# A decoder step on one NeuronCore: other orders ahead of the expert loop (sample numerators, gate rows, per-layer-embedding turns)

## Chip, cores and metric

The kernel runs on one core of one Trainium2 chip. The metric is the device time of one execution in microseconds (us), the median of several runs. All data are float32 in HBM.

## The reference, cut to what matters

One layer of a hybrid decoder for 512 prompt tokens and 8 x 8 sample tokens (576 tokens, width 1024): an mLSTM mixer with 4 heads beside a pooling mixer, then 64 routed experts (8 per token) and one shared, then a per-layer embedding (PLE) behind a gate.

```python
def _layer(x, p, C0, n0, m0, buf0, start_pos, ...):
    h = _rmsnorm(x, norm_mix_g)
    z = h @ w_in                                   # q, k, v, o, gates i and f, u
    i_pre = z[..., g0:g0+H] + b_igate;  log_f = log_sigmoid(z[..., g0+H:g0+2*H] + b_fgate)
    h_a, C, n, m = _mlstm(q * DH**-0.5, k, v, i_pre, log_f, C0, n0, m0)
    h_a = headnorm(h_a) * head_norm_g * sigmoid(o)
    h_b, buf = _pool_mixer(u, buf0, start_pos, w_pool, pool_scale)
    x = x + concat(h_a, h_b) @ w_out
    x = x + _moe(_rmsnorm(x, norm_ffn_g), ...)     # 64 experts of (1024x256, 1024x256, 256x1024), top 8
    gate = sigmoid(_rmsnorm(x, norm_ple_g) @ w_ple_gate)
    return x + (p @ w_ple_proj) * gate, C, n, m, buf
# _mlstm, for a token t after a stored state (C0, n0, m0), the sample tokens' case:
#   num = w_inter * (q C0) + (scores * decay) v ;  nq = w_inter * (q n0) + rowsum(scores * decay)
#   h = num / max(|nq|, exp(-m_t)) ;  C = fw * C0 + sum_s iw_s k_s v_s
```

## The kernel before, in words

The program is written out by hand, engine by engine (SyncE issues loads and stores, GpSimd, ScalarE, VectorE, TensorE), with semaphores between them. Ahead of the expert loop TensorE's work is a list of groups. Each group of matrix products fills one of the eight PSUM banks, and one engine, VectorE ("v") or ScalarE ("s"), drains it. `psum_groups` lists all groups in the order in which TensorE fills them; group n has bank n mod 8 (`free_bank` waits until group n-8 is drained, `full_bank` until group n is filled), and `drain` asserts that each engine drains its groups in the order of the list. So an order is changed in three places: the list, TensorE's program and the draining engine's program.

The stages ahead of the loop, as far as the change touches them:

- 0 to 19 us. x comes in by five tiles (four of 128 tokens, one of 64), is turned (`x1T`), and ScalarE and GpSimd work out rstd of each token and diagonals of it. A product of ones with the diagonals spreads rstd over all partitions: `rB` 0 for the prompt tiles, `rB` 1 for the sample tile (L2003). Then come the gate rows `g` (L2012) and q, k, u (L1978), whose weights come through a ring of two chunks of 2 MB. VectorE waits for both spreads and then works the gate rows out ahead of its drains of q.
- 199 to 230 us. Behind the prompt's numerators `num`: `Ms` (rows spread over partitions, L2088), `Ss` (the sample scores), the turns of k (`kn`, L2098) and `kns`, the turn `n0` of the stored normaliser, the prompt states `Cp` (L1978, 128x129), which need k weighted by VectorE (L1475), the turns of the gated heads (`haT`, L2111), which need `head_out` on VectorE (L1502, L1504), and the output product `wo` (L1978, 128x512). VectorE's chain in front of `head_out` goes over GpSimd once (L908). The sample numerators `nS` (L2201, 72 pairs of instructions) need only `Ms`, `Ss`, `n0` and the loaded states; they stand behind `wo`(0,1), the last prompt state and the third `haT`. ScalarE copies them and takes four squares. After `wo`(0,1) the norm of x2 tile 0 runs over ScalarE, GpSimd and VectorE (L1299), and `turn_x`(0) (L1973) on TensorE waits for it.
- 318 to 343 us. The router has chosen the experts of each token. From sorted positions VectorE builds one-hots (L1733 to L1753), a product with them picks the rows of one loop step (`pick`, L2269), VectorE turns this into row numbers (`first_index`, L1768 to L1778), and GpSimd gathers the rows from HBM by four indirect DMAs (L994). VectorE transposes the gathered rows (`turned_rows`, L1786). In between run the shared expert's first products of tiles 2 and 3 (`first`, L2155), its product on GpSimd or, for the last tile, on VectorE (L1810), the turns of that (`turn_h`, L2164), and ten transposes of the PLE input (`pT`, L2291), which ScalarE drains (L1172) once `s_order` is 2, as their target holds routing data until then. SP loads the third expert's weights (home 4: `mixpj`, `wide`, L666 and L670), whose place holds the PLE input, after the last `pT` drain; home 3 (`xT`) after the last `first`(3).
- The loop: 46 steps of up to 128 gathered rows, each with one to two experts. A step's first product (L2314, L2319) needs the transposed rows and the weights; its end releases a place for the next expert's weights (3 MB each). TensorE enters it when the last eight groups are drained, `pk` 2 (VectorE) and `shT` 3 (ScalarE) among them. The tail after it holds the PLE gate and the final norm.

## Time and profile before

| | us |
|---|---|
| median of 3 runs | 1022.5 |
| lowest and highest | 1021.36, 1022.6 |
| the profiled execution | 1020.37 |
| its span | 1018.3 |
| mean granted TensorE clock, share of full | 0.984 |
| TensorE busy | 959.6 |
| VectorE, ScalarE, GpSimd busy | 426.8, 146.4, 344.5 |
| DMA moved | 297.50 MB, mean 292 GB/s |

Times in the rows are microseconds from the start of the span. A row of a timeline is: start, duration, engine, line, operation, output <- input, shape, count, and in brackets the idle time of the engine ahead of it with what released it. PE is TensorE's matmul, PEld its weight load, DVE VectorE, ACT ScalarE, POOL GpSimd, SPq a DMA issued by SyncE. A row of the windows is: stretch and its length; busy time and instructions of PE, PEld, DVE, ACT and POOL; granted clock; DMA share; GB/s. A row of the chain of waits is: start, duration, what was on the chain. Each TensorE product of float32 makes two rows of count.

### The profile page before, as it was taken

What the parts mean: (1) busy time and instruction counts of PE and PEld (TensorE: products, weight loads), DVE (VectorE), ACT (ScalarE), POOL (GpSimd) and SP (SyncE); (2) the same over time, 40 slices, a digit from 0 to 9 for tenths busy, and PEclk for the clock granted to TensorE, in tenths of its full rate; (3) what the DMA queues carried; (4) which work ended last, traced back from release to release, by engine and by line L of the source; (5) the groups of instructions that cost most, each with busy time, mean ns of one, the idle gap of its engine ahead of it and who ended that gap; (6) DMA issues with size and microseconds to landing.
All of it is one profiled execution on the core that took longest, in us unless ns stands there. A gap on an engine that the chain in (4) does not pass through costs nothing.

```text
span 1018.3 us, 16186 instructions
## 1 busy us (share of the span) xinstructions
PE 959.6 (94%) x5994; PEld 420.7 (41%) x5994; DVE 426.8 (42%) x1215; ACT 146.4 (14%) x358; POOL 344.5 (34%) x439
## 2 busy tenths in 40 slices
PE   7999999999999899999999998989997899989996
PEld 5777655555554433233222333323332223333442
DVE  3411222344578543344343342333424243432885
ACT  4000023401011101010110000000100001102332
POOL 6000321310143644444344443334433344440132
PEclk9999999999999899999999999999998999999998
DMA  8032214222067999999999999999999999988932
GB/s 275 10 94 104 83 63 131 85 73 64 38 235 275 362 349 399 411 409 413 412 413 413 405 415 413 410 393 397 411 410 399 380 409 411 412 328 341 421 136 83
DMA packets 76115, 297.50 MB, mean 292 GB/s; under 512 B 15622, under 2 KB 26062, under 8 KB 49149
## 3 DMA queue, kind: packets, MB, share of 16 engines
q1 hardware_dynamic: 60133, 258.68, 65.0%
q0 software_dynamic: 15904, 37.79, 9.7%
q8 instruction: 48, 0.79, 0.3%
q14 instruction: 30, 0.25, 0.1%
HBM read 276.56 MB, written 31.50 MB: 303 GB/s over the span
## 4 chain that ended last, share of the span: by engine, by line
PE 64%; DMA 22%; DVE 5%; issue 4%; POOL 3%; DVEq 1%; SPq 1%; ACT 1%; POOLq 0%; ACTq 0%
PE bank L1978 22%; PE bank L2319 18%; DMA arena<-in_ex_w 9%; PE bank L2314 7%; DMA arena<-xs_dram,slot 6%; PE bank L2414 5%; DMA ring<-in_ex_w 5%; PE bank L1984 2%; PE bank L2155 2%; POOL arena L994 2%; DMA arena<-y_dram 1%; PE bank L2082 1%; PE bank L2072 1%; DMA x<-in_x_prompt 1%; PE bank L2119 1%
## 5 line engine op out<-in xcount | busy, mean ns | idle before, releaser
L2319 PE MATMUL bank<-arena 128*32 128x512 f32 x1440 | 270.4, 608 | 10.6 <-issue 4.7
L994 POOL DMA_INDIRECT arena<-xs_dram,slot x192 | 204.8, 1066 | 73.1 <-issue 62.3
L2319 PE MATMUL bank<-ring,arena 128*32 128x512 f32 x864 | 212.2, 605 | 5.8 <-DMA arena<-in_ex_w 5.8
L1010 POOL DMA_INDIRECT y_dram<-arena,outrow x46 | 47.1, 1023 | 270.3 <-DVE slot L1772 214.3
L2319 PE MATMUL bank<-xT,arena 128*32 128x512 f32 x576 | 114.7, 604 | 5.5 <-DMA ring<-in_ex_w 5.5
L2319 PEld LDWEIGHTS bank<-arena 128*32 128x32 f32 x1440 | 68.0, 112 | 112.5 <-issue 104.3
L1786 DVE STREAM_TRANSPOSE arena<-arena 128x1024 f32<-128x1024 f32 x48 | 59.7, 1244 | 87.2 <-DMA arena<-xs_dram,slot 87.1
L1978 PE MATMUL bank<-xT,ring 128*128 128x288 f32 x384 | 93.4, 407 | 0.0
L2319 PE MATMUL bank<-mixpj,arena 128*32 128x512 f32 x384 | 86.4, 599 | 0.0
L1978 PEld LDWEIGHTS bank<-xT,ring 128*128 128x128 f32 x384 | 73.0, 190 | 20.4 <-DMA ring<-in_w_in 0.5
L2319 PEld LDWEIGHTS bank<-ring,arena 128*32 128x32 f32 x864 | 51.0, 111 | 49.9 <-issue 43.9
L1851 DVE SCALAR_TENSOR_TENSOR arena<-bank,gate,arena 128x256 f32<-128x256 f32 x46 | 22.2, 484 | 110.8 <-ACT arena L1204 110.7
L1832 DVE COPY outrow<-yrow 128x1 int32<-128x1 int32 x46 | 7.1, 154 | 146.8 <-PE bank L2319 117.6
L1204 ACT ACTIVATE arena<-bank 128x256 f32<-128x256 f32 x46 | 17.7, 384 | 345.1 <-PE bank L2319 259.4
L1978 PE MATMUL bank<-ring,mixpj 128*128 128x512 f32 x128 | 56.7, 597 | 0.8 <-issue 0.8
L1978 PE MATMUL bank<-ring,xT 128*128 128x512 f32 x128 | 56.1, 593 | 0.0
L2414 PE MATMUL bank<-ring,xT 128*128 128x512 f32 x128 | 55.7, 593 | 0.4 <-DVE xT L1903 0.4
L2314 PE MATMUL bank<-ring,arena 128*128 128x512 f32 (+1 forms) x112 | 51.9, 614 | 1.3 <-DVE arena L1786 1.3
L1200 ACT COPY arena<-bank 128x512 f32<-128x512 f32 x46 | 27.0, 587 | 174.7 <-PE bank L2319 137.1
L2314 PE MATMUL bank<-arena 128*64 128x512 f32 x144 | 50.2, 596 | 0.7 <-DVE arena L1833 0.6
L2319 PEld LDWEIGHTS bank<-xT,arena 128*32 128x32 f32 x576 | 29.1, 111 | 50.2 <-issue 43.4
L886 POOL TENSOR_TENSOR arena<-arena 128x710 f32<-128x710 f32 (+3 forms) x10 | 13.9, 1394 | 94.7 <-DVE arena L1391 87.8
(417 smaller groups left out, 1242.5 us busy)
## 6 DMA issues: line engine op xcount, KB each, us to landing
arena<-in_ex_w SPq DMA_DIRECT2D x78, 1024.0 KB, 21.7
ring<-in_ex_w SPq DMA_DIRECT2D x50, 1024.0 KB, 20.4
xT<-in_ex_w SPq DMA_DIRECT2D x28, 1024.0 KB, 19.1
mixpj<-in_ex_w SPq DMA_DIRECT2D x24, 1024.0 KB, 20.1
arena<-y_dram SPq DMA_DIRECT2D x18, 1024.0 KB, 11.0
wide<-in_ex_w SPq DMA_DIRECT2D x12, 1024.0 KB, 25.4
ring<-in_w_in SPq DMA_DIRECT2D x5, 2048.0 KB, 8.2
ring<-in_w_out SPq DMA_DIRECT2D x2, 2048.0 KB, 8.5
```

Source lines behind the costliest of these rows:

```text
L994: pool.indirect_dma_start(xg[b][:, 256 * a:256 * a + 256], None, xs_quarter, bass.IndirectOffsetOnAxis(slot[k][:, a:a + 1], 0), bounds_che ...
L1010: pool.indirect_dma_start(y_dram, bass.IndirectOffsetOnAxis(outrow[b][:, 0:1], 0), og[b], None, bounds_check=K * T - 1, oob_is_err=False). ...
L1200: act.copy(og[b][:, 0:512], bank[5][:, :]).then_inc(s_out0, 1)
L1204: act.activation(hs, bank[2][:, 0:FF], ACT.Silu).then_inc(s_silu, 1)
L1786: dve.transpose(xgT[b][:, :, :].rearrange("p c (a t) -> p a c t", t=32), xg[b].rearrange("p (a c t) -> p a c t", c=KT, t=32)).then_inc(s_x ...
L1851: dve.scalar_tensor_tensor(out=hh, in0=bank[2][:, FF:2 * FF], scalar=gate[depth(j)][:, 0:1], in1=hs, op0=ALU.mult, op1=ALU.mult).then_inc( ...
L1978: ins = pe.matmul(b, lhs(c), rhs(c), start=(c == 0), stop=(c == nk - 1))
L1984: pe.matmul(b[0:NS, 0:n], lhs(c), rhs0(c), start=(c == 0), stop=(c == nk - 1))
L2155: ins = pe.matmul(b[0:r, :], xT[:, c, tok(i)], sw13[:, :, c, :], start=(c == 0), stop=(c == KT - 1))
L2314: ins = pe.matmul(b[t, :], lhs[:, t], rhs(home(p)), start=start, stop=stop)
L2319: ins = pe.matmul(b[t, :], lhs[:, t], rhs(home(own if lane < 3 else common)), start=start, stop=stop)
L2414: ins = pe.matmul(bank[AT["gt", i, n] % 8][0:r, :], xT[:, c, tok(i)], w[:, c, :], start=(c == 0), stop=(c == KT - 1))
```

## The change

Three reorderings. No instruction is added or removed.

1. The gate rows `g` come between the two spreads `rB` 0 and `rB` 1.
2. `n0` is turned and drained ahead of `Ms`. `nS` comes right behind `kns`, ahead of the prompt states; of `Ss` it waits only ahead of its last step. The turn of k 3 and prompt state 2 come ahead of `wo`(0,0). ScalarE copies and squares `nS` ahead of the prompt states; VectorE weights k 3 ahead of `head_out`(1).
3. The five `pT` groups come ahead of the first pick, and ScalarE drains them ahead of the turn of the sample tile's shared product. The last `first`(3) is cut after three of eight products instead of two. VectorE transposes the first gathered rows (`turned_rows(64, 0)`) ahead of its shared product of the last tile and of `first_index(2)`, instead of behind them.

```diff
--- before.py
+++ after.py
@@ -41,7 +41,7 @@
     g = [(("g1",), "v")]
     for i in range(NT):
         g += [(("x1T", i, 0), "v"), (("x1T", i, 1), "v")]
-    g += [(("rB", 0), "s"), (("rB", 1), "s"), (("g",), "v")]
+    g += [(("rB", 0), "s"), (("g",), "v"), (("rB", 1), "s")]
     g += [(("q", j, n), "v") for j in range(H) for n in range(2)]
     g += [(("k", j, n), "v") for j in range(H) for n in range(2)]
     g += [(("u", j, n), "v") for j in range(H) for n in range(2)]
@@ -57,7 +57,7 @@
         if h == 0:
             g += [(("o", NT - 1), "s")]
         g += [(("num", h, i), "s") for i in range(4)]
-    g += [(("Ms", 0), "v"), (("Ms", 1), "v"), (("Ss",), "v")]
+    g += [(("n0",), "v"), (("Ms", 0), "v"), (("Ms", 1), "v"), (("Ss",), "v")]
 
     def halves(key, i, e):
         return [((key, i, n), e) for n in range(1 if i == NT - 1 else 2)]
@@ -68,19 +68,19 @@
     def state(h):
         return [(("C", h, c), "v") for c in range(3)]
 
-    g += [(("kn", 0), "v"), (("kn", 1), "v"), (("kns",), "s"), (("n0",), "v")]
+    g += [(("kn", 0), "v"), (("kn", 1), "v"), (("kns",), "s"), (("nS",), "s")]
     g += [(("Cp", 0), "s"), (("Cp", 1), "s"), (("kn", 2), "v"), (("haT", 0), "v")]
-    g += [(("wo", 0, 0), "v"), (("kn", 3), "v"), (("Cp", 2), "s"), (("haT", 1), "v")]
-    g += [(("wo", 0, 1), "v"), (("Cp", 3), "s"), (("haT", 2), "v"), (("nS",), "s")]
+    g += [(("kn", 3), "v"), (("Cp", 2), "s"), (("wo", 0, 0), "v"), (("haT", 1), "v")]
+    g += [(("wo", 0, 1), "v"), (("Cp", 3), "s"), (("haT", 2), "v")]
     g += [(("wo", 1, 0), "v")] + turned(0) + [(("haT", 3), "v"), (("wo", 1, 1), "v")] + state(0) + [(("r", 0), "s")]
     g += [(("wo", 2, 0), "v")] + turned(1) + [(("haT", 4), "v")] + state(1)
     g += [(("wo", 2, 1), "v")] + state(2) + [(("r", 1), "s")]
     g += [(("wo", 3, 0), "v")] + turned(2) + state(3) + [(("wo", 3, 1), "v"), (("r", 2), "s")]
     g += [(("wo", 4, 0), "v")] + turned(3) + [(("nout",), "s"), (("r", 3), "s")] + turned(4)
     g += [(("sh", 0), "s"), (("r", 4), "s"), (("sh", 1), "s"), (("shT", 0), "s"), (("sh", 4), "s"), (("pos",), "v")]
-    g += [(("shT", 1), "s"), (("ord",), "v"), (("sh", 2), "s"), (("pk", 0), "v"), (("shT", 4), "s")]
+    g += [(("shT", 1), "s"), (("ord",), "v"), (("sh", 2), "s")]
     g += [(("pT", i), "s") for i in range(NT)]
-    g += [(("pk", 1), "v"), (("sh", 3), "s"), (("shT", 2), "s"), (("pk", 2), "v"), (("shT", 3), "s")]
+    g += [(("pk", 0), "v"), (("shT", 4), "s"), (("pk", 1), "v"), (("sh", 3), "s"), (("shT", 2), "s"), (("pk", 2), "v"), (("shT", 3), "s")]
 
     def norm3(a):
         return [(("x3T", tail[a], 0), "v"), (("x3T", tail[a], 1), "s")] if a < NT else []
@@ -1132,9 +1132,6 @@
                 drain("s", act.copy(hTs[i], b[:, 0:2 * P].rearrange("p (c t) -> p c t", t=P)[:, :, 0:r]),
                       "shT", i)
 
-            for h in range(H):
-                state(h)
-            square2(0)
             b = full_bank(act, "nS")
             for n in range(2):
                 ins = act.copy(nbs.rearrange("p (a l) e -> p l a e", l=2)[:, n],
@@ -1145,6 +1142,9 @@
                 act.activation(junk[0:NS, 0:P], nbs[:, h, 0:P], ACT.Square, accum_out=fac[0:NS, 0, NP_, h:h + 1]
                                ).then_inc(s_sqh, 1)
                 act.wait_ge(s_sqh, H * NP_ + h + 1)
+            for h in range(H):
+                state(h)
+            square2(0)
             x2t(0)
             for i in range(1, NP_):
                 square2(i)
@@ -1163,7 +1163,6 @@
             sh(2)
             sht(1)
             sh(3)
-            sht(NP_)
             for i in range(NT):
                 b = full_bank(act, "pT", i)
                 if i == 0:
@@ -1171,6 +1170,7 @@
                 r = ROWS[i]
                 drain("s", act.copy(pT(i), b[:, 0:2 * P].rearrange("p (c t) -> p c t", t=P)[:, :, 0:r]),
                       "pT", i)
+            sht(NP_)
             sh(4)
             sht(2)
             sht(3)
@@ -1538,6 +1538,9 @@
                     dve.wait_ge(s_xsd[i % 2], 16 * (i // 2))
                 normalise_quarters(i, xs2[i % 2], g_b, NT)
 
+            b = full_bank(dve, "n0")
+            dve.wait_ge(s_c0, 16 * (NB + 1))
+            drain("v", dve.tensor_copy(C0[:, :, :, P], b[:, 0:NB * H].rearrange("p (b h) -> p b h", h=H)), "n0")
             dve.wait_ge(s_qzero, 1)
             for k in range(2):
                 b = full_bank(dve, "Ms", k)
@@ -1557,16 +1560,13 @@
             drain("v", dve.tensor_tensor(PTs, b[0:NS, 0:H * NS].rearrange("p (h t) -> p h t", t=NS), Ds, ALU.mult), "Ss")
             weighted_k(0)
             weighted_k(1)
-            b = full_bank(dve, "n0")
-            dve.wait_ge(s_c0, 16 * (NB + 1))
-            drain("v", dve.tensor_copy(C0[:, :, :, P], b[:, 0:NB * H].rearrange("p (b h) -> p b h", h=H)), "n0")
             factors(0, P, 0, NP_)
             head_out(0)
             weighted_k(2)
             turn_ha(0)
+            weighted_k(3)
             head_out(1)
             add_half("wo", 0, 0)
-            weighted_k(3)
             turn_ha(1)
             head_out(2)
             dve.wait_ge(s_gb, 16)
@@ -1805,11 +1805,11 @@
             link(dve.tensor_reduce(np_f[0:1, 2:3], np_c[:, 0:PASSES - 1], AX.X, ALU.add))
             dve.tensor_copy(np_i[0:1, 1:2], np_f[0:1, 2:3])
             dve.tensor_scalar(np_i[0:1, 0:1], np_f[0:1, 2:3], 1.0, None, ALU.add).then_inc(s_np, 1)
+            turned_rows(64, 0)
             dve.wait_ge(s_silu_sh, NT)
             after(dve, "shT", 2)
             dve.tensor_tensor(hh, hu, hs, ALU.mult).then_inc(s_hsh, 1)
             first_index(2)
-            turned_rows(64, 0)
             one_hots(0, 0, 3, heads[4], None)
             turned_rows(64, 1)
             heads += [expert(AHEAD - 1)]
@@ -1995,7 +1995,8 @@
             for i in range(NT):
                 pe.wait_ge(s_x[i], 16)
                 turn("x1T", i, x[:, i, :])
-            for n, tiles in enumerate((range(NP_), (NP_,))):
+            def spread_rstd(n, tiles):
+
                 b = free_bank(pe, "rB", n)
                 for k, i in enumerate(tiles):
                     r = ROWS[i]
@@ -2003,6 +2004,7 @@
                     ins = pe.matmul(b[:, P * k:P * k + r], onesf[0:r, :], diag[0:r, i, 0:r], start=True, stop=True)
                 ins.then_inc(filled, 1)
 
+            spread_rstd(0, range(NP_))
             wait_drained(pe, "x1T", NT - 1, 0)
             wait_drained(pe, "x1T", NT - 1, 1)
             pe.wait_ge(s_wg, 32)
@@ -2012,6 +2014,7 @@
                     ins = pe.matmul(b[NS * n:NS * n + 36, 0:TH], wg[:, c, :], xT[:, c, TH * n:TH * n + TH],
                                     start=(c == 0), stop=(c == KT - 1))
             ins.then_inc(filled, 1)
+            spread_rstd(1, (NP_,))
             for name in ("q", "k", "u"):
                 chunk_in(pe, name)
                 w = chunk(name).rearrange("p (c n) -> p c n", n=512)
@@ -2081,6 +2084,9 @@
                         at = BLK[j] + P * (i - j)
                         ins = pe.matmul(b[:, 0:DE], PT[:, at:at + P], v[:, j, h, :], start=(j == 0), stop=(j == i))
                     ins.then_inc(filled, 1)
+            pe.wait_ge(s_c0, 16 * (NB + 1))
+            b = free_bank(pe, "n0")
+            pe.transpose(b[:, 0:NB * H], n0nat, ident[0:NB * H, 0:NB * H]).then_inc(filled, 1)
             W = 2 * NS + NB
             for k in range(2):
                 b = free_bank(pe, "Ms", k)
@@ -2170,28 +2176,13 @@
             for h in range(H):
                 ins = pe.transpose(b[0:NS, P * h:P * h + P], kT[:, h, SEQ:T], ident[:, :])
             ins.then_inc(filled, 1)
-            pe.wait_ge(s_c0, 16 * (NB + 1))
-            b = free_bank(pe, "n0")
-            pe.transpose(b[:, 0:NB * H], n0nat, ident[0:NB * H, 0:NB * H]).then_inc(filled, 1)
-            prompt_state(0)
-            prompt_state(1)
-            turn_k(2)
-            turn_ha(0)
-            wait_drained(pe, "mix", H - 1, 1)
-            wait_drained(pe, "haT", 0)
-            wo(0, 0)
-            turn_k(3)
-            prompt_state(2)
-            turn_ha(1)
-            wo(0, 1)
-            prompt_state(3)
-            turn_ha(2)
-            wait_drained(pe, "Ss")
-            wait_drained(pe, "n0")
+            wait_drained(pe, "Ms", 1)
             b = free_bank(pe, "nS")
             for pair in range(2):
                 col = slice(DE * pair, DE * pair + DE)
                 for k in range(NB + 1):
+                    if k == NB:
+                        wait_drained(pe, "Ss")
                     for n in range(2):
                         h = 2 * pair + n
                         if k < NB:
@@ -2200,6 +2191,19 @@
                             lhs, rhs = PTs[:, h, :], v[0:NS, NP_, h, :]
                         ins = pe.matmul(b[NS * n:NS * n + NS, col], lhs, rhs, start=(k == 0), stop=(k == NB))
             ins.then_inc(filled, 1)
+            prompt_state(0)
+            prompt_state(1)
+            turn_k(2)
+            turn_ha(0)
+            turn_k(3)
+            prompt_state(2)
+            wait_drained(pe, "mix", H - 1, 1)
+            wait_drained(pe, "haT", 0)
+            wo(0, 0)
+            turn_ha(1)
+            wo(0, 1)
+            prompt_state(3)
+            turn_ha(2)
             wait_drained(pe, "haT", 1)
             wo(1, 0)
             turn_x(0)
@@ -2281,8 +2285,6 @@
                 b = free_bank(pe, "pk", j)
                 pick(j + 1, j % 2, b, j, j > 0).then_inc(filled, 1)
 
-            first_pick(0)
-            turn_h(NP_)
             pe.wait_ge(s_p, 16 * NT)
             for i in range(NT):
                 r = ROWS[i]
@@ -2290,9 +2292,11 @@
                 for c in range(2):
                     ins = pe.transpose(b[:, P * c:P * c + r], ptile[0:r, i, P * c:P * c + P], ident[0:r, 0:r])
                 ins.then_inc(filled, 1)
-            first(3, 0, 2)
+            first_pick(0)
+            turn_h(NP_)
+            first(3, 0, 3)
             first_pick(1)
-            first(3, 2, KT)
+            first(3, 3, KT)
             turn_h(2)
             first_pick(2)
             turn_h(3)
```

## Rows read from the trace of the kernel before

**Rows 1.** Page, part 2: DMA busy tenths in 40 slices of 25.5 us.

```profile
DMA  8032214222067999999999999999999999988932
```

**Rows 2.** Windows of ten us.

```profile
320.00:330.00 10.00, 8.11 (x29) 3.48 (x28) 9.16 (x23) 1.14 (x4) 6.17 (x7) 0.98 0.40 164
...
360.00:370.00 10.00, 10.00 (x80) 3.84 (x80) 4.24 (x14) 1.25 (x3) 3.40 (x3) 1.00 0.92 343
```

**Rows 3.** Timeline of TensorE and its weight loads, 14 to 20 us.

```profile
14.71 0.40 PE L2003 MATMUL bank<-arena,onesf 64*128 64x64 f32 x2 [1.06 <-POOL arena L812]
15.05 4.08 PE L2012 MATMUL bank<-xT,arena 128*36 128x288 f32 x32
...
19.05 1.51 PEld L1978 LDWEIGHTS bank<-xT,ring 128*128 128x128 f32 x7 [0.46 <-DMA ring<-in_w_in]
```

**Rows 4.** Timeline, 203 to 209 us; the last row is of the chain.

```profile
203.45 2.05 PE L1978 MATMUL bank<-arena 128*128 128x129 f32 x16 [1.49 <-DVE arena L1475]
...
206.47 0.69 DVE L1504 SCALAR_TENSOR_TENSOR arena<-arena 128x512 f32<-128x512 f32 x1
...
207.21 0.66 PE L2111 MATMUL bank<-ident,arena 128*128 128x128 f32 x4 [1.27 <-DVE arena L1504]
...
208.70 0.67 PE L1978 MATMUL bank<-ring,mixpj 128*128 128x512 f32 x1 [0.83 <-issue]
...
225.77 4.56 PE bank L2201 x72
```

**Rows 5.** Timeline of VectorE, and the turn in the chain, 228 to 238 us.

```profile
228.88 2.28 DVE L1299 SCALAR_TENSOR_TENSOR arena<-x,rstd,wide 128x128 f32<-128x128 f32 x8
...
237.39 0.87 PE bank L1973 x8
```

**Rows 6.** Timeline of all engines, 329 to 343 us.

```profile
329.20 0.27 PE L2269 MATMUL bank<-arena 128*128 128x24 bf16 x5 [1.64 <-DVE arena L1739]
...
329.67 2.37 PE L2291 MATMUL bank<-ident,mixpj 128*128 128x128 f32 x10
...
332.08 0.27 ACT L1172 COPY pTs<-bank 128x128 f32<-128x128 f32 x1
...
332.34 0.25 DVE L1739 TENSOR_TENSOR arena<-arena 128x90 bf16<-128x90 f32 x1
...
332.53 0.83 SPq L666 DMA_DIRECT2D mixpj<-in_ex_w  x2
...
334.59 5.41 PE L2155 MATMUL bank<-arena,xT 128*128 128x512 f32 x12
...
335.24 0.99 POOL L994 DMA_INDIRECT arena<-xs_dram,slot  x1 [0.30 <-issue]
...
340.76 0.43 DVE L1810 TENSOR_TENSOR arena<-arena 128x256 f32<-128x256 f32 x1 [1.07 <-ACTq L1127]
...
341.50 0.99 POOL L994 DMA_INDIRECT arena<-xs_dram,slot  x1 [0.30 <-issue]
...
341.70 1.24 DVE L1786 STREAM_TRANSPOSE arena<-arena 128x1024 f32<-128x1024 f32 x1
...
341.72 0.37 ACT L1132 COPY xT<-bank 128x256 f32<-128x256 f32 x1 [0.55 <-PE bank L2164]
...
342.99 3.47 PE L2314 MATMUL bank<-ring,arena 128*128 128x512 f32 x4 [1.31 <-DVE arena L1786]
```

**Rows 7.** Windows of one us, columns as in rows 2.

```profile
331.00:332.00 1.00, 1.00 (x7) 0.55 (x5) 0.97 (x5) 0.89 (x3) 1.00 (x1) 0.50 0.03 8
...
345.00:346.00 1.00, 1.00 (x2) 0.34 (x1) 0.00 (x0) 0.00 (x0) 0.73 (x1) 0.50 1.00 381
```

**Rows 8.** Timeline of VectorE; the last row is of the chain.

```profile
349.32 1.25 DVE L1786 STREAM_TRANSPOSE arena<-arena 128x1024 f32<-128x1024 f32 x1 [5.22 <-DMA arena<-xs_dram,slot]
...
393.59 9.52 DMA arena<-xs_dram,slot
```

**Rows 9.** DMA issues: count, KB each, median us to landing.

```profile
xs_dram<-arena SPq DMA_DIRECT2D x4, 512.0 KB, 2.6
```

## The prediction, made before the changed kernel had run

> **What bounds the kernel now.** I read the page first. The DMA digits [rows 1] fall into two parts: low and patchy over the first thirteen slices (to 331 us), then nines to 891 us. In those the expert weights stream at nearly the full rate, and the loop cannot be shorter than that stream. Ahead of it the windows by stretch [rows 2] show TensorE full and the DMA engines partly idle: 0.40 busy from 320 to 330 us. From 360 to 370 us, in the loop's first steps, the DMA share is 0.92, so there the stream still waits for TensorE's steps to release its buffers one by one. The start of the first loop step therefore moves the stream behind it one for one: a microsecond won ahead of 343 us is won at the end, unless the first step starts late for another reason. Next I went through TensorE's timeline ahead of 343 us and looked for the waits in square brackets, since only they can be removed by another order. They stand at three places, one for each part of the change.
>
> **Part 1, the gates between the two spreads of rstd.** The small spread waits 1.06 us for GpSimd's last diagonal, and the gate product follows for 4.08 us [rows 3]. With the gates first, they cover that wait, and the spread (0.40) comes after them. But the q product behind them starts at 19.05 with its weight load released by the DMA of its weights after a 0.46 us wait [rows 3]: the weights land then, whatever the order. The bounds are 0 and the full 1.06; I take 0, because that weight-load row names the DMA. VectorE now needs the small spread's copy for the gate rows, but it needed the gates anyway, which came last before. Its drains of q stand behind that chain; the chain starts no later.
>
> **Part 2, sample numerators (nS) ahead of the prompt states.** Three waits of TensorE go: 1.49 us ahead of the first prompt state (weighted k from VectorE), 1.27 us ahead of the turn of the first head output, and 0.83 us ahead of the first output product (the turned heads have to be drained): 3.59 us [rows 4]. They are waits on one chain of VectorE and GpSimd, which ends with head output 0 at 207.2 us (L1504 [rows 4]). The work moved into its place is 4.56 us long [rows 4], starts at about 202.0 (203.45 less the wait of 1.49), needs the Ms banks (drained before the first of the waits) and is done by 206.5. The two prompt states (2.05 us [rows 4]) follow to 208.5, and only then does TensorE ask for weighted k and head 0, long ready. One short wait appears: k 2 is now turned at 209.1 and has to be scaled (0.7 us on VectorE) before prompt state 2; the turns of head 0 and of k 3, some 0.9 us, cover it to about 0.2. The turn of n0 goes from a hole to ahead of Ms and pushes the chain by at most 0.25. I take 3.59 less 0.1: **3.5 us earlier**, between 3.1 and 3.7.
>
> What is late next: nS was also the cover between the end of wo(0,1) and the turn of x2 tile 0. The norm of x2 tile 0 starts at 228.88 and takes 2.28, and the turn comes at 237.39 [rows 5], a slack of 6.2 us. Without nS there it is 6.2 − 4.56 = 1.6, less some 0.3 for the copy of prompt state 3 and the two VectorE pieces in front: 1.0 to 1.3 us left. Covered; if it weren't, the excess would come straight off the 3.5. ScalarE's copies of the prompt states now stand behind its nS copies and four squares; the first who asks for such a bank is wo(0,1), by the sum above some 10 us after they could start. SP's queue has nothing that waits longer: its waits are on groups that come no later.
>
> **Part 3, PLE turns ahead of the first pick.** TensorE waits 1.64 us ahead of the first pick for the one-hots of VectorE, and the ten PLE transposes behind it take 2.37 us [rows 6]. In the order after, they run in that hole. Their 2.37 us are at a granted clock of 0.50 (1.2 GHz) [rows 7], which came after the wait; eight transposes of the same shape took 0.87 at 1.0 [rows 5], so ten take 1.1 and fit in: the first pick stays at 329.20. The products of tile 3 then start some 2.4 us earlier, pick 1 waits for its one-hots until about 332.7 (written at 332.34 to 332.59 [rows 6]), and the last ten of the 16 products, at 5.41 us for twelve [rows 6], end near 337.5, not 340.0. This alone looks like 2.5 us. It isn't, because the first loop step does not wait for TensorE: it starts at 342.99, released by VectorE's transposition of the gathered rows at 341.70 [rows 6]. The gather's last piece is issued by GpSimd at 335.24 and takes 1 us, and that issue rests on the first pick, which stays. So the start of the loop is set by when the gather lands, plus what VectorE has behind it.
>
> And there the change adds two things. First, the waits on PLE drains: the last one ends at 332.35, and SP issues home 4's load (3 MB) at 332.53 [rows 6]. It now goes out 2.1 us earlier, ahead of all four pieces of the gather and not only of the last three. Second, the transposition is moved ahead of the shared expert's last product on VectorE (L1810). Before, that product, the turn of it and ScalarE's copy ran from 340.76 to 342.09 while the gather was on its way [rows 6]. Now VectorE stands at the gather's semaphore with the product, the index of pick 2 and the one-hots queued behind it, and TensorE's turn of tile 3 and the bank waits at the loop's head wait for these.
>
> The landing isn't in the trace directly; it is bounded by who waits. This gather needs at most 341.70 − 336.23 = 5.5 us from its last issue. The next one made VectorE wait 5.22 us until 349.32 [rows 8]; with its last issue ended at 342.49 it took 6.8. In the saturated loop one took 9.52 [rows 8]. From below: the stores of 0.5 MB to xs_dram took 2.6 us to land [rows 9]. I take 5.0: near the first row, as home 4's load, begun earlier, is also further along. Then: 336.2 + 5.0 = 341.2, VectorE starts at 341.3; transposition 1.24; then L1810 to the end of ScalarE's copy, 342.09 − 340.76 = 1.33; 0.1 for TensorE's wake (an estimate; it took 0.05 in [rows 6]). The first step starts at 344.0, in the old frame, against 342.99: **1.0 us later**. With 2.6 us it starts at 341.6 (1.4 earlier), with 6.8 at 345.8 (2.8 later), with 9.5 at 348.5 (5.5 later). The step's own dip of the clock (0.50 at 345 [rows 7]) follows the idle time ahead of it as before; as the idle time is longer, it may cost up to 0.5 more, kept in the range.
>
> The Trainium skill has a rule that speaks against my reading (DMA: Bandwidth & Descriptors, Queues, rings and completion order): each DMA engine takes turns between the queues it has work for, a packet at a time. By it a load that is issued first doesn't hold a gather back; that is the second case below. The 9.52 us of [rows 8] speak against a full share for the gather, though not against taking turns.
>
> Home 3's load goes out earlier by as much as the last product of tile 3 ends earlier. It is worth nothing: at 360 to 370 us the engines idle again [rows 2] and wait for the steps.
>
> **The sum.** −0 − 3.5 + 1.0 = −2.5 us on the profiled execution (1020.37 us, of which 1018.3 are the span): 1017.9. The median shown is 2.1 above it, so the forecast for the median is 1022.5 − 2.5 = **1020.0 us**.
>
> **The rivals.**
> 1. As forecast: part 2 whole, the gather late and serial. Its own range is −1.5 to −4: 1018.5 to 1021. Chance 0.42.
> 2. The gather is not held back (landing 2.6 to 4 us after issue). Then the serial VectorE piece costs nothing: −3.5 − 1.4 = −4.9, 1017.6 us, and with part 1's bound as far as 1016.5. For it: piece 1 now also runs while little else is in flight. Against: the 6.8 of the next gather. Chance 0.23.
> 3. The load fully ahead of it holds it back like the next gather, 6.8 us: −3.5 + 2.8 = −0.7, 1021.8 us. The change then only swaps a wait of TensorE for one of VectorE. Chance 0.23.
> 4. Slower: all four pieces queue behind home 4's load as in the saturated loop, 9.5 us, and VectorE holds the last shared product behind them: −3.5 + 5.5 = +2.0, with 0.5 for the longer low clock +2.5, 1025.0 us. It decides from a landing 9.6 us after the last issue. For it: the load leads all four pieces now. Against: only 3 MB are queued here, while the loop has loads without end. Chance 0.08.
> 5. Part 2 does not do what it says, since another wait follows (the norm of tile 0, or a bank held by the late copies): half of the 3.5 is lost, −0.7 again. Chance 0.04.
>
> **From these to the numbers.** Gains and losses ahead of the loop go through a saturated stream whose waits fall a little differently each time, which I put at 1 us to either side. About 0.2% (2 us) is what a measurement of this kernel can tell from no change. Faster by more: three quarters of the first case, nearly all of the second, a little of the third, 0.56. Within: 0.33. Slower: 0.11, the fourth case and the tails of the third. The range reaches from the second case's 1017.6 less 1 to the third's 1021.8 plus 1: 1016.6 to 1022.9; it leaves the fourth out.
>
> **What would show it.** Right: nS begins at about 202 and TensorE has no wait between 202 and 226 above 0.3 us; q starts at 19.05 as before; the first pick is at 329.2 less 3.5, no clock of 0.50 follows it; home 4's load is issued 5.6 us earlier on the clock; VectorE waits for the gather and TensorE then waits some 5 us ahead of its first step, at about 340.5. Wrong: a first step before 339 (the second case) or after 342 (the third, the fourth); a wait at the turn of x2 tile 0 (the fifth); or a loop that does not follow its first step one for one.

## The result and the profile after

| | before | after |
|---|---|---|
| median, same chip (6 runs each), us | 1021.69 | 1016.81 |
| lowest and highest | 1020.94, 1022.6 | 1016.51, 1018.5 |
| the profiled execution | 1020.37 | 1016.82 |
| its span | 1018.3 | 1014.8 |
| mean granted clock | 0.984 | 0.983 |

The ratio is 0.9948 [0.9935, 0.9960]: 4.1 to 6.6 us less. The forecast was 1020.0, 2.5 less than the 1022.5 of its three runs of before. The direction and the range held; the size was out by a factor of two. The two spans differ by 3.5 only, since the profiled execution of before was 1.3 us under its own median.

The rows of after that answer to rows 1 and 2, the page's DMA digits, then the windows of the same stretches:

```profile
DMA  9033214222177989999999999999999999988932
```

```profile
320.00:330.00 10.00, 9.27 (x45) 4.66 (x44) 8.49 (x33) 2.29 (x8) 4.79 (x5) 1.00 0.42 145
360.00:370.00 10.00, 10.00 (x95) 3.09 (x97) 4.24 (x14) 1.25 (x3) 5.59 (x5) 1.00 0.89 338
```

**Part 1.** Timeline of TensorE and its weight loads, against rows 3. q starts at 18.39, not 19.05. Its weights still end the wait, 0.66 us earlier than before:

```profile
13.23 4.08 PE L2014 MATMUL bank<-xT,arena 128*36 128x288 f32 x32
17.23 0.43 PE L2004 MATMUL bank<-arena,onesf 64*128 64x64 f32 x2
18.39 1.97 PE L1978 MATMUL bank<-xT,ring 128*128 128x288 f32 x7 [0.73 <-DMA ring<-in_w_in]
```

**Part 2.** Timeline of TensorE, 200 to 212 us, against rows 4. The sample numerators (L2192) start at 201.11; no row up to the first output product (209.93) has a wait. The first and the last of L2192's four rows stand here.

```profile
201.11 1.98 PE L2192 MATMUL bank<-arena,xT 128*64 128x129 f32 x32
...
205.30 0.44 PE L2192 MATMUL bank<-arena 64*64 64x129 f32 x4
205.66 2.05 PE L1978 MATMUL bank<-arena 128*128 128x129 f32 x16
207.55 0.60 PE L2104 MATMUL bank<-ident,arena 128*128 128x128 f32 x4
207.99 0.60 PE L2117 MATMUL bank<-ident,arena 128*128 128x128 f32 x4
208.43 0.60 PE L2104 MATMUL bank<-ident,arena 128*128 128x128 f32 x4
208.94 1.16 PE L1978 MATMUL bank<-arena 128*128 128x129 f32 x8
209.93 2.31 PE L1978 MATMUL bank<-ring,mixpj 128*128 128x512 f32 x5
```

Against rows 5, the norm of x2 tile 0 on VectorE and its turn on TensorE. The norm ends at 230.97, the turn comes at 232.31, without a wait: a slack of 1.3 us.

```profile
228.71 2.26 DVE L1299 SCALAR_TENSOR_TENSOR arena<-x,rstd,wide 128x128 f32<-128x128 f32 x8
...
232.31 1.04 PE L1973 MATMUL bank<-ident,arena 128*128 128x128 f32 x8
```

**Part 3.** Timeline of all engines, 322 to 343 us, against rows 6 and 8:

```profile
322.49 1.30 PE L2293 MATMUL bank<-ident,mixpj 128*128 128x128 f32 x10
324.31 0.27 PE L2273 MATMUL bank<-arena 128*128 128x24 bf16 x5 [0.52 <-DVE arena L1739]
325.06 0.83 SPq L666 DMA_DIRECT2D mixpj<-in_ex_w  x2
330.34 1.00 POOL L994 DMA_INDIRECT arena<-xs_dram,slot  x1 [0.30 <-issue]
336.24 1.25 DVE L1786 STREAM_TRANSPOSE arena<-arena 128x1024 f32<-128x1024 f32 x1 [3.27 <-DMA arena<-xs_dram,slot]
337.40 0.38 DVE L1811 TENSOR_TENSOR arena<-arena 128x256 f32<-128x256 f32 x1
337.84 0.69 PE L2170 MATMUL bank<-ident,arena 128*128 128x128 f32 x2 [4.76 <-DVE arena L1811]
338.57 0.37 ACT L1132 COPY xT<-bank 128x256 f32<-128x256 f32 x1 [4.77 <-PE bank L2170]
339.43 4.76 PE L2318 MATMUL bank<-ring,arena 128*128 128x512 f32 x7 [0.90 <-ACT xT L1132]
...
342.70 1.25 DVE L1786 STREAM_TRANSPOSE arena<-arena 128x1024 f32<-128x1024 f32 x1 [3.04 <-DMA arena<-xs_dram,slot]
```

The PLE turns run at the full clock in the hole. VectorE waits for the gather, which is there 4.9 us after its last issue ended at 331.34, and TensorE waits 4.8 us for VectorE. The first step starts at 339.43, 3.56 us before that of rows 6. Against rows 7, the windows of one us: no 0.50 behind the PLE turns, and the dip of the first step as before.

```profile
331.00:332.00 1.00, 1.00 (x3) 0.38 (x2) 0.93 (x3) 0.00 (x0) 0.97 (x2) 1.00 0.90 373
...
340.00:341.00 1.00, 1.00 (x2) 0.33 (x1) 0.00 (x0) 0.00 (x0) 0.70 (x2) 0.50 1.01 394
```

### The profile page after: what moved, and what is told of

Same layout as the page of the kernel before. It is cut to its first block, busy times and chain, and to the rows that moved or that the text cites. A ratio compares the mean times of both kernels' runs of the same rounds, so it can differ in the third digit from the quotient of the medians.

```text
span 1014.8 us, 16186 instructions
## 1 busy us (share of the span) xinstructions
PE 958.8 (94%) x5994; PEld 418.5 (41%) x5994; DVE 426.6 (42%) x1215; ACT 145.9 (14%) x358; POOL 344.0 (34%) x439
## 4 chain that ended last, share of the span: by engine, by line
PE 63%; DMA 23%; DVE 5%; issue 4%; POOL 2%; SPq 1%; DVEq 1%; ACT 0%; POOLq 0%; ACTq 0%
PE bank L1978 22%; PE bank L2323 19%; DMA arena<-in_ex_w 9%; PE bank L2318 8%; DMA arena<-xs_dram,slot 6%; PE bank L2418 5%; DMA ring<-in_ex_w 5%; PE bank L1984 2%; POOL arena L994 2%; DMA arena<-y_dram 1%; DMA ring<-in_w_in 1%; PE bank L2161 1%; PE bank L2085 1%; PE bank L2075 1%; PE bank L2125 1%
```

## The experiments

The first theory, A: the end follows the first loop step one for one, and each part has the size that the traces of before and after give it. The rival, B: the forecast's sizes hold and the rest is scatter. Later rivals stand with their runs. The kernels ran in four groups, each on a chip of its own and beside runs of before on it (e0 to e3, then e5, e6, e9, e10, then e12 to e15, then e16 to e18), all noisier than the first chip. So I read four landmarks from each trace, whose differences are steadier than the end: the start of q, from there the turn of x2 tile 0, from the first pick the first loop step, and from the last gather issue's end the first transposition. A difference of means below has a 95% interval by resampling the runs. From x2 tile 0 to the first pick it was 91.98 to 92.02 us in every trace.

| kernel | median us (before) | ratio to before, interval | q at | q to x2 tile 0 | first pick to first step | last gather issue to transposition |
|---|---|---|---|---|---|---|
| before, first trace | 1021.69 | | 19.05 | 218.17 | 13.79 | 5.5 |
| after, first trace | 1016.81 (1021.69) | 0.9948 [0.9935, 0.9960] | 18.39 | 213.92 | 15.12 | 4.9 |
| e0_before | 1025.67 (1024.62) | 1.0008 [0.9988, 1.0027] | 19.77 | 218.18 | 14.99 | 6.7 |
| e1_gates | 1023.03 (1024.62) | 0.9988 [0.9972, 1.0004] | 18.72 | 218.17 | 14.42 | 6.1 |
| e2_nums | 1022.34 (1024.62) | 0.9959 [0.9941, 0.9977] | 19.86 | 213.91 | 15.24 | 6.7 |
| e3_ple | 1026.12 (1024.62) | 1.0014 [0.9996, 1.0033] | 18.60 | 219.88 | 15.07 | 4.8 |
| e10_after | 1020.87 (1025.99) | 0.9953 [0.9932, 0.9974] | 18.08 | 213.91 | 15.13 | 4.9 |
| e5_product_first | 1017.76 (1025.99) | 0.9931 [0.9907, 0.9954] | 18.27 | 213.91 | 13.17 | 4.8 |
| e6_hold4 | 1018.24 (1025.99) | 0.9931 [0.9910, 0.9953] | 19.22 | 213.91 | 11.80 | 1.6 |
| e9_dve_only | 1026.51 (1025.99) | 1.0011 [0.9995, 1.0027] | 20.30 | 218.19 | 15.79 | 5.5 |
| e14_after | 1021.10 (1025.02) | 0.9958 [0.9944, 0.9973] | 18.77 | 213.92 | 15.20 | 4.9 |
| e12_no_late | 1019.07 (1025.02) | 0.9943 [0.9925, 0.9961] | 18.41 | 213.92 | 14.37 | 6.0 |
| e13_no_late_hold | 1017.83 (1025.02) | 0.9936 [0.9921, 0.9951] | 17.29 | 213.91 | 12.36 | 3.9 |
| e15_product_turn_hold | 1017.66 (1025.02) | 0.9937 [0.9919, 0.9954] | 17.19 | 213.91 | 11.67 | 2.4 |
| e18_both_again | 1017.59 (1022.10) | 0.9960 [0.9943, 0.9978] | 18.73 | 213.92 | 11.68 | 2.4 |
| e16_hold_two | 1023.42 (1022.10) | 1.0007 [0.9995, 1.0019] | 18.56 | 213.91 | 11.71 | 2.4 |
| e17_n0_behind | 1020.83 (1022.10) | 0.9990 [0.9977, 1.0003] | 18.66 | 217.92 | 15.07 | 4.8 |

The last column is the landing where VectorE waited for the gather (4.8 and 4.9, and 5.5 in e9_dve_only), and an upper bound elsewhere.

### Each part alone

**e0_before**, no edit:

> The kernel before once more, for a second trace of its loop and for how far two traces of one program differ. Both theories expect a ratio of 1.000. The theory that the loop follows its first step one for one expects the first loop step within 0.3 us of 342.99, and the profiled time may still differ by a microsecond or two through the waits inside the loop, as the shift between the two traces at hand wanders from 0.9 to 5.1 us inside the loop.

It came out at 1.0008, which is the noise. Its landmarks matter more: q 0.72 us later than in the first trace of before, the first step 1.20 later from the first pick, with not one line changed. So the first trace of before was an early one at two places.

**e1_gates**, part 1 alone:

```diff
-    g += [(("rB", 0), "s"), (("rB", 1), "s"), (("g",), "v")]
+    g += [(("rB", 0), "s"), (("g",), "v"), (("rB", 1), "s")]
...
+            spread_rstd(0, range(NP_))
...
+            spread_rstd(1, (NP_,))
```

> Part 1 alone. Theory A (the end follows the first loop step one for one, each part is worth its shift of that step): q starts at about 18.4 instead of 19.05, everything behind is 0.66 us earlier, ratio 0.9994. Theory B (the forecast's): q starts when its weights land, nothing moves, ratio 1.000. Both the same if the weights land later than 18.4 in this run.

q starts at 18.72 and waits for its weights, as in after. The end is 0.9988, 1.2 us less; the interval reaches zero. The five traces with the old order of gates have q at 18.60 to 20.30, always directly behind the gate product. The rows of e0_before, TensorE then its weight loads:

```profile
15.44 0.40 PE L2003 MATMUL bank<-arena,onesf 64*128 64x64 f32 x2 [1.06 <-POOL arena L812]
15.77 4.08 PE L2012 MATMUL bank<-xT,arena 128*36 128x288 f32 x32
...
19.77 1.27 PEld L1978 LDWEIGHTS bank<-xT,ring 128*128 128x128 f32 x6 [0.46 <-DMA ring<-in_w_in]
```

The idle time of 0.46 is the same as in rows 3 although everything is 0.72 later. In e2_nums, e3_ple and e9_dve_only the same 0.46 is put down to "issue". So the weights had landed, and the 0.46 goes with the gate product and not with the data.

**e2_nums**, part 2 alone:

```diff
-    g += [(("kn", 0), "v"), (("kn", 1), "v"), (("kns",), "s"), (("n0",), "v")]
+    g += [(("kn", 0), "v"), (("kn", 1), "v"), (("kns",), "s"), (("nS",), "s")]
...
+            wait_drained(pe, "Ms", 1)
             b = free_bank(pe, "nS")
```

> Part 2 alone. Theory A: TensorE's start of wo(1,0) moves from 230.25 to about 226.1, the first loop step by the same 4.1 to 4.2 us, the time by 4.2 us, ratio 0.9959. Theory B (the forecast's size, 3.5 us): 0.9966. Theory C (part 3's earlier loads bring a share of the result, beside the first step): the same as A here, and a ratio above that of the whole change (0.9948) by 0.001 at least.

From q to the turn of x2 tile 0 it is 213.91 against 218.17: 4.26 us. The end, 0.9959 [0.9941, 0.9977], is 4.2 less.

**e3_ple**, part 3 alone:

```diff
+            turned_rows(64, 0)
             dve.wait_ge(s_silu_sh, NT)
             after(dve, "shT", 2)
             dve.tensor_tensor(hh, hu, hs, ALU.mult).then_inc(s_hsh, 1)
             first_index(2)
-            turned_rows(64, 0)
```

with the PLE turns and drains moved ahead and `first(3)` cut at three.

> Part 3 alone. Theory A (the end follows the first loop step): the first pick stays at 329.2, the first loop step comes 1.3 us later than 342.99, the time is 1.3 us longer, ratio 1.0013. Theory C (the loads of homes 4 and 3, which go out 2 to 2.7 us earlier, shorten the stream although the first step is late): the first step is late by the same 1.3 us, yet the time is 0.7 to 1.4 us shorter, ratio 0.9987 to 0.9993.

The end is 1.0014, 1.4 more. Of this trace 1.7 us have nothing to do with part 3: x2 tile 0 comes 219.88 after q. The waits of rows 4 are all there in that kernel, and behind them the granted clock fell to 0.50 (1.2 GHz), windows of e3_ple:

```profile
205.00:209.00 4.00, 1.89 (x11) 1.09 (x10) 3.67 (x7) 0.27 (x1) 0.05 (x1) 0.95 1.04 211
209.00:212.00 3.00, 3.00 (x5) 1.23 (x4) 0.48 (x1) 0.00 (x0) 0.00 (x0) 0.50 0.08 15
```

The three ratios multiply to 0.9961; the whole change had 0.9948, 0.9953 and 0.9958 on three chips. Within these intervals the parts add up, and theory B's −2.5 us (0.9976) is outside the interval of each of these three.

### What the late part costs

**e10_after** and **e14_after** are the changed kernel again, one beside each of two groups.

> The changed kernel once more, beside the kernel before and the runs of this call, as their common mark. Theory A (the end follows the first loop step one for one; 0.66 to 1.0 us from the gates, 4.25 from the numerators, 0.1 to 1.3 lost by the late part) gives 3.6 to 4.8 us less than before, a ratio of 0.9953 to 0.9965. Theory B (the forecast's sizes) gives 2.5 us less, 0.9976. First step about 15.1 us after the first pick, the transposition of the first gathered rows released 4.8 to 5.0 us after the last gather issue ends.

> The changed kernel once more, as the mark for this call: ratio to before 0.9948 to 0.9960, first step 15.1 us after the first pick, transposition 4.9 us after the last gather issue ends.

Both came as expected: 15.13 and 15.20 us from pick to step, the landing at 4.9.

**e5_product_first**, after with VectorE's old order at one place:

```diff
-            turned_rows(64, 0)
             dve.wait_ge(s_silu_sh, NT)
             after(dve, "shT", 2)
             dve.tensor_tensor(hh, hu, hs, ALU.mult).then_inc(s_hsh, 1)
             first_index(2)
+            turned_rows(64, 0)
```

> The changed kernel, but VectorE keeps its order of before at one place: the shared expert's last product and the index of pick 2 come ahead of the first transposition, not behind it. Theory A: what the late part costs is that serial tail alone, since the gather still lands 4.9 us after its last issue; the product runs while the gather is on its way, the first step follows the transposition's end by 0.1 instead of 1.95 us, so it starts 13.2 us after the first pick instead of 15.1, and the whole is 1.9 us shorter than the changed kernel (1.5 to 2.2), 5.5 to 6.7 shorter than before. Rival F (the tail is only a part, the stream behind it is bound elsewhere): the first step starts 1.9 earlier, yet the end moves by less than 0.5, as later steps wait for gathers or weights. Rival G (the gather lands later when VectorE is not waiting at it): the first step is not earlier, and nothing is won.

VectorE and TensorE of e5_product_first; the product is done while the gather is on its way:

```profile
333.27 0.43 DVE L1810 TENSOR_TENSOR arena<-arena 128x256 f32<-128x256 f32 x1 [0.43 <-issue]
336.05 1.25 DVE L1786 STREAM_TRANSPOSE arena<-arena 128x1024 f32<-128x1024 f32 x1 [1.76 <-DMA arena<-xs_dram,slot]
...
337.35 8.83 PE L2318 MATMUL bank<-ring,arena 128*128 128x512 f32 x16 [3.16 <-DVE arena L1786]
```

The first step is 1.96 us earlier from the pick, by theory A's number. The median is 3.1 below the changed kernel of the same group; the difference of the means is 2.4, with an interval of 0.9 to 3.9. F's "under 0.5" and G fall. The product also starts 9.1 us after the first pick (324.18) here, where it came after 11.6 in the order of before: the 2.5 us that the forecast saw for TensorE are real, but the landing takes most of them.

**e9_dve_only**, the other way round, before with that one edit:

```diff
+            turned_rows(64, 0)
             dve.wait_ge(s_silu_sh, NT)
...
             first_index(2)
-            turned_rows(64, 0)
```

> The kernel before with one edit of the late part alone: VectorE transposes the first gathered rows ahead of the shared expert's last product. Theory A: this is the whole cost of the late part. The tail from the transposition's end to the first step grows from 0.1 to about 1.95 us, so the first step starts 15.6 us or so after the first pick (13.8 to 15.2 in the order of before), and the whole is 1.3 to 1.9 us longer than before, 1.0013 to 1.0019. Rival (the late part's cost lies in the earlier load, not in VectorE's order): within 0.3 us of before.

15.79 us from pick to step, and 1.0011: 1.1 us more, under the 1.3 expected, and the interval reaches zero. From the transposition's start to the first step it is 3.2 us in this order and 1.3 in the old one; the old order's own late steps (14.99 in e0_before) make the difference at the end smaller than the tail.

**e6_hold4**, after with home 4's load held:

```diff
             wait_drained(sp, "pT", NT - 1)
+            sp.wait_ge(s_hsh, 4)
             load13(home(4), f)
```

> The changed kernel, but the load of home 4 (3 MB) waits until the shared expert's last product is done on VectorE, so that it is issued behind all pieces of the first gathers; now the product stands behind the first transposition, so the load goes out some 12 us later. Theory H (the load ahead holds the gather back, the forecast's reason for its 5.0 us): the first gather lands 2.6 to 4 us after its last issue, and the first step starts 1 to 2.3 us earlier. Theory A: the load ahead does not hold it back; the landing is 4.8 us or later (up to 6.7, as in the runs with the order of before), and the first step is not earlier. For the end the load's own 8.7 us at 343 GB/s come later by some 12 us: if the third expert's step waits for them, the end is 1 to 5 us later than the changed kernel's; if the stream catches up, within 1.

As built, the wait is on the fourth shared product, GpSimd's, which stands right behind the first gather's four issues; the load goes out 8.0 us after the first pick instead of 0.7, so 7.3 later and not 12. GpSimd and VectorE of e6_hold4:

```profile
331.17 1.00 POOL L995 DMA_INDIRECT arena<-xs_dram,slot  x1 [0.30 <-issue]
333.73 1.22 DVE L1787 STREAM_TRANSPOSE arena<-arena 128x1024 f32<-128x1024 f32 x1
...
344.52 1.25 DVE L1787 STREAM_TRANSPOSE arena<-arena 128x1024 f32<-128x1024 f32 x1 [7.37 <-issue]
```

The transposition has no wait: the gather was there at most 1.6 us after its last issue. Theory H is right and theory A wrong: the load ahead does hold the gather back, by 3.3 us or more. The first step is 3.3 us earlier than in the changed kernel, the end 2.4 by the means (1.2 to 3.5); the second transposition now comes late, 6.5 us after its gather's last issue. e9_dve_only fits in: there the load went out 4.5 us ahead of the last issue's end, not 6.3 as in the changed kernel, and the gather landed at 5.5, not 4.9.

**e12_no_late** is parts 1 and 2 without part 3, **e13_no_late_hold** the same with the load held:

> Parts 1 and 2 without the late part 3. Theory A (part 3 costs 1.33 us, as the first two traces show): the first step comes 13.8 us after the first pick, and the whole is 1.3 us shorter than the changed kernel. Theory J (part 3 is worth nothing either way on the mean: in the runs with its late order the first step came 13.8, 14.4, 15.0, 15.2 us after the first pick, since the gather there landed 5.5 to 6.7 us after its last issue): within 0.6 us of the changed kernel.

> Parts 1 and 2 without part 3, but the load of home 4 waits for the fourth shared product on GpSimd, that is until all pieces of the first gather are issued. Theory H (a load on the DMA engines holds the gather back, in the order of before too): the gather is there 1.5 us after its last issue, before VectorE comes to it; the first step then waits for TensorE's products of tile 3 and the last shared product, 12.9 us after the first pick, and the whole is 0.9 to 2.3 us shorter than parts 1 and 2 alone. Rival: a landing of 5 us or more as before, and no gain.

e12_no_late has 14.37 from pick to step. Its median is 2.0 below the changed kernel's, the means 1.4 (from 3.3 less to 0.5 more), so at the end A and J are not told apart. The rows tell why the old order scatters. TensorE's third pick and VectorE in e12_no_late, then VectorE in e0_before:

```profile
335.32 0.27 PE L2279 MATMUL bank<-arena 128*128 128x12 bf16 x5
335.90 0.43 DVE L1810 TENSOR_TENSOR arena<-arena 128x256 f32<-128x256 f32 x1 [1.08 <-issue]
336.80 0.17 DVE L1768 TENSOR_REDUCE token<-bank 128x4 f32<-128x8 f32 x1 [0.47 <-PE bank L2279]
...
337.40 1.23 DVE L1786 STREAM_TRANSPOSE arena<-arena 128x1024 f32<-128x1024 f32 x1
```

```profile
342.85 0.17 DVE L1768 TENSOR_REDUCE token<-bank 128x4 f32<-128x8 f32 x1 [0.91 <-PE bank L2164]
...
343.63 1.24 DVE L1786 STREAM_TRANSPOSE arena<-arena 128x1024 f32<-128x1024 f32 x1
```

The transposition follows VectorE's index of pick 2 without a wait for the gather. So in the old order the gather had landed, and the last column of the table is an upper bound there. What set the first step was a chain through TensorE: its last product of tile 3, ScalarE's two pieces on it, VectorE's shared product (L1810), the index (L1768 and what follows it), the transposition. L1810 started 11.56 to 11.65 us after the first pick in all five traces of the old order (before, e0, e1, e2, e12). The scatter is in the index behind it: no idle time in the first trace of before, 0.46 and 0.47 in e1_gates and e12_no_late, 0.91 in e0_before and e2_nums. The third pick, which the bracket names, had ended 1.2 us before the index started, so what the index waits for is not shown.

e13_no_late_hold has 12.36 (12.9 expected); its means are 2.9 below the changed kernel's (1.6 to 4.2). Its gather was there within 3.9 us, but that is not what brought the first step forward. Windows behind the first pick, e12_no_late and then e13_no_late_hold:

```profile
325.00:328.00 3.00, 3.00 (x12) 2.03 (x11) 2.64 (x12) 1.92 (x6) 1.57 (x2) 0.52 0.01 3
```

```profile
324.00:327.00 3.00, 3.00 (x22) 1.69 (x21) 2.52 (x11) 1.41 (x6) 1.69 (x2) 1.00 0.01 3
```

The granted clock stayed at 1.00 behind the wait ahead of the first pick, where it fell to 0.50 in the six other traces with the old TensorE order; neither kernel had issued the load when the two clocks parted. So L1810 started 10.0 us after the pick instead of 11.6, and the index followed it 0.5 us sooner, which accounts for the 2.0 us that the first step is earlier than in e12_no_late. That trace shows no gain at the first step by the held load. Its means are 1.5 us below those of e12_no_late (from 3.1 less to 0.1 more).

### Where the rest of the gain goes

**e15_product_turn_hold**, after with both repairs, and again as **e18_both_again**:

```diff
             wait_drained(sp, "pT", NT - 1)
+            sp.wait_ge(s_hsh, 4)
             load13(home(4), f)
...
-            turned_rows(64, 0)
             dve.wait_ge(s_silu_sh, NT)
             after(dve, "shT", 2)
             dve.tensor_tensor(hh, hu, hs, ALU.mult).then_inc(s_hsh, 1)
+            turned_rows(64, 0)
             first_index(2)
```

> The changed kernel with both repairs: VectorE does the last shared product first, then the transposition, then the index of pick 2; home 4's load waits until the first gather is issued. If landing and serial tail are the two costs of part 3, the transposition starts 9.4 us after the first pick without a wait, ends at 10.7, and the first step starts 10.9 to 11.1 us after the first pick (15.1 in the changed kernel), when ScalarE's last copy is done too. The whole is 3.3 to 4.1 us shorter than the changed kernel if the end follows one for one, and 0.6 to 0.9 shorter than with the held load alone (ratio to before about 0.992). Rival F (the stream behind takes part of it back, since the third expert's weights come 8 us later): 2 to 3 us shorter than the changed kernel, no better than either repair alone.

> The kernel with both repairs once more, as the mark of this call: ratio to before 0.992 to 0.9955, first step 11.7 us after the first pick, then a wait of 3.6 us ahead of the first turn of that step, for one-hots that stand on VectorE behind the second gather's transposition.

The first step comes 11.7 us after the pick, 3.5 us earlier than in the changed kernel but 0.6 to 0.8 later than expected: TensorE enters the loop only when the index of pick 2 is drained, and that now stands behind the transposition (see the bracket of the first row below). The end has 2.8 less by the means (1.1 to 4.4), no more than one repair gives, as rival F had it. TensorE and VectorE of e18_both_again: the first turn of step 0 (L2371) waits for one-hots that stand on VectorE behind the second transposition, and that one waits for the second gather, held by the loads let go at 332.70.

```profile
336.34 7.13 PE L2319 MATMUL bank<-ring,arena 128*128 128x512 f32 x16 [1.66 <-DVE gate L1777]
343.92 1.25 DVE L1787 STREAM_TRANSPOSE arena<-arena 128x1024 f32<-128x1024 f32 x1 [6.74 <-DMA arena<-xs_dram,slot]
347.30 0.50 PE L2371 MATMUL bank<-ident,arena 128*128 128x128 f32 x2 [3.60 <-DVE arena L1852]
```

**e16_hold_two**, the loads held until the second gather has landed:

```diff
             wait_drained(sp, "pT", NT - 1)
-            sp.wait_ge(s_hsh, 4)
+            sp.wait_ge(s_gather[1], 64)
             load13(home(4), f)
```

> As the kernel with both repairs, but the load of home 4 (and that of home 3 behind it) waits until the second gather has landed too, some 15 us later than in the changed kernel instead of 8. Theory K (in the kernel with both repairs the loads, once let go, held the second gather back, and that took back what the first had won): the second gather lands 1.5 to 2.5 us after its last issue instead of 6.0, the wait of 3.6 us falls to under 0.5, the first turn of step 0 comes 20.7 to 21.5 us after the first pick (22.6), and the end is another 1.5 us or more earlier than with both repairs. Theory F (the stream is the bound from its start, so each microsecond in which the DMA engines stand idle is lost): the end is 3 us or more later than with both repairs, even where the first two steps are earlier, and some step between 3 and 8 waits for its weights.

Both theories were right, each for its stretch. VectorE and TensorE of e16_hold_two:

```profile
339.81 1.25 DVE L1787 STREAM_TRANSPOSE arena<-arena 128x1024 f32<-128x1024 f32 x1 [2.55 <-DMA arena<-xs_dram,slot]
344.31 0.50 PE L2371 MATMUL bank<-ident,arena 128*128 128x128 f32 x2 [0.77 <-DVE arena L1852]
357.28 0.63 PE L2324 MATMUL bank<-xT,arena 128*32 128x512 f32 x3 [0.41 <-DMA xT<-in_ex_w]
472.21 1.07 PE L2324 MATMUL bank<-xT,arena 128*32 128x512 f32 x3 [4.53 <-DMA ring<-in_ex_w]
```

The second gather lands 1.8 us after its last issue ended at 337.97 (K), and the first turn of step 0 comes 2.8 us earlier from the pick than in e18_both_again. But the end is 5.8 us later by the medians and 5.0 by the means (4.1 to 5.8), as F had it: in the eleventh step TensorE waits 4.53 us for weights, where e18_both_again has no wait. That is later than the steps 3 to 8 that I had named. The loads went out 7.5 us later from the pick than in e18_both_again, and most of it is missing at the end.

**e17_n0_behind**, after with n0's turn and drain in their old place:

```diff
-    g += [(("n0",), "v"), (("Ms", 0), "v"), (("Ms", 1), "v"), (("Ss",), "v")]
+    g += [(("Ms", 0), "v"), (("Ms", 1), "v"), (("Ss",), "v")]
...
+            wait_drained(pe, "n0")
             b = free_bank(pe, "nS")
```

> The changed kernel, but the stored normaliser n0 is turned and drained where it was before, behind the turn of the sample keys and, on VectorE, behind the weighting of k 0 and 1; the sample numerators wait for it. By the trace of the changed kernel the drain then ends 203.4 us into the span, where the numerators start at 201.1: TensorE waits 2.3 us. If the hole of 3.6 us is what part 2 fills and no more, x2 tile 0 is turned 2.0 to 2.4 us later after q's start than the 213.9 us of the changed kernel, and the end is 2.0 to 2.4 us later: a ratio to before of 0.9972 to 0.9983. Rival: the wait is hidden (the numerators' later start only uses up slack), and it costs under 0.5.

The wait came as expected, 2.27 us; the cost didn't: 217.92 from q to x2 tile 0, 4.00 more. TensorE and windows of e17_n0_behind:

```profile
203.81 3.02 PE L2193 MATMUL bank<-arena,xT 128*64 128x129 f32 x32 [2.27 <-DVE arena L1562]
207.39 2.25 PE L2193 MATMUL bank<-arena,xT 128*64 128x129 f32 x32
209.94 2.05 PE L1978 MATMUL bank<-arena 128*128 128x129 f32 x16
```

```profile
204.00:207.00 3.00, 3.00 (x34) 2.67 (x33) 1.56 (x3) 0.00 (x0) 1.10 (x1) 0.60 1.04 238
207.00:209.00 2.00, 2.00 (x28) 1.67 (x28) 0.00 (x0) 0.00 (x0) 0.00 (x0) 0.75 1.05 212
```

Behind the wait the clock fell (0.60 and 0.75 in these windows), and the numerators took 6.13 us from their start to the first prompt state instead of 4.55: 1.58 more. With the start 2.43 later that makes 4.0. The end is 0.9990, against 0.9948 to 0.9958 with n0 ahead.

## Why the forecast was right in direction and wrong in size

- **How far it was off.** The gain was 4.9 us by the medians and not 2.5. Of the 2.4 between them, by the means below, 1.2 are part 1, 0.8 part 2 and 0.4 part 3. The time itself, 1016.81, lies 3.2 under the forecast, since the median of before was also 0.8 lower in the six new runs than in the three old ones.
- **Part 1, taken at 0: this step failed.** It rested on one bracket, the DMA named at q's weight load in rows 3. The same 0.46 us stands in traces where q comes 0.72 us later: q followed the gate product, and the weights had landed. With the gates first, q waits for its weights in all but one of twelve traces. It starts at 18.36 on their mean (17.19 to 19.22), against 19.52 on the mean of five with the old order (18.60 to 20.30): 1.2 us, or 1.0 without e9_dve_only, whose gate product was slow. The forecast's upper bound was 1.06. The run of part 1 alone says 1.2 too, with an interval that reaches zero.
- **Part 2, 3.5 forecast, 4.26 measured, within 0.03 wherever the clock stayed.** The mechanism was right: the hole was filled, and no wait came in its place. The three waits' 3.59 us were the right rows but not the whole hole. Ahead of each wait the last piece also ran out its full duration, where otherwise the next one overlaps it: a group of four transposes takes 0.60 us but 0.44 from start to start (207.55, 207.99 and 208.43 above). By rows 4 and the timeline around them that is 0.16 + 0.22 + 0.15 = 0.53, in sum 4.12 of the 4.26. That working is an argument; the sum is measured. The short wait of 0.1 ahead of prompt state 2 did not come.
- **The slack at x2 tile 0, 1.0 to 1.3 forecast, was 1.3**, and no wait stood there.
- **Part 3, +1.0 forecast.** The landing was right: 5.0 us forecast, 4.9 measured. That the load ahead holds the gather back was right too (1.6 or less and 1.8 without it). The serial tail was 1.43 in the forecast (1.33 and 0.1) and 1.94 measured from the transposition's end (337.49) to the step (339.43). The turn of the product took 0.69 us and not 0.44, as the clock was at 0.50 by then, and TensorE began 0.49 us after ScalarE's copy had ended (338.94), not 0.1. What failed is the reading of before: "the first loop step does not wait for TensorE". It did. The gather had landed, and the chain was TensorE's last product of tile 3, ScalarE, L1810, the index, the transposition. That chain gave 13.8 to 15.2 us from pick to step (mean 14.56 of five), the new order 15.07 to 15.20. The cost is 1.33 against the first trace and 0.6 on the mean. The two bounds lay close together: the transposition came 5.5 us after the last issue in the first trace of before, and 5.5 is also the landing that e9_dve_only shows.
- **The sum on means:** −1.2 − 4.3 + 0.6 = −4.9 us, and the medians of the first chip differ by 4.9. That close an agreement is partly luck, as q's mean alone is uncertain by some tenths. On the first two traces it is −0.66 − 4.25 + 1.33 = −3.6, and the spans differ by 3.5. The forecast subtracted its terms from one execution that was early at q (0.5 us) and at the first step (0.8 us).
- **"The loop follows its first step one for one"** holds within the noise for after against before, where the weights' loads kept their distance from the steps or went out earlier. It fails where a load is held long: e16_hold_two gained 2.8 us at the first turn and lost 5.0 to 5.8 at the end. Where it was held for 7.3 us (e6_hold4), 3.3 at the first step became 2.4 at the end, and the interval (1.2 to 3.5) holds both.
- **The rivals.** The time came where the second one lay (1017.6), but by another way: its mechanism, a gather not held back, did not occur. That the range, drawn down to 1016.6 for that rival, held the result by 0.2 us is luck. Of the third, 6.8 us of landing, only the second gather shows something near (5.5 to 7.0). The fourth, 9.5, did not occur. By the rule of the Trainium skill that the prediction weighed (DMA: Bandwidth & Descriptors, Queues, rings and completion order), a DMA engine takes turns between its queues, so an earlier load need not hold a gather back. The runs of this case show that it did here, 4.9 us against 1.6 or less; how the engines shared their time between the two, no run shows.

The late part is the change's weak place. Either repair, VectorE's product first or home 4's load behind the first gather, was 2.4 us faster than the changed kernel on the same chip, and both together 2.8, not told apart from one. Parts 1 and 2 alone with the load held do as well (2.9), though their trace shows no gain that the held load brought. What isn't settled: whether part 3 in its own form costs 0.6 or more at the end (e12_no_late's interval holds zero), why the index of pick 2 waits longer in some traces of the old order, and why the clock stayed up behind the first pick in one trace of seven.
